# Gate and up products of the feed-forward stages: one 512-column matmul over the tokens' high and low parts instead of two of 256

## What is computed

```python
def rmsnorm_2(x, g):
    xf = x.astype(jnp.float32)
    y = xf * lax.rsqrt(jnp.mean(xf * xf, axis=-1, keepdims=True) + EPS)
    return (y * g.astype(jnp.float32)).astype(x.dtype)

def swiglu(h, wg, wu, wd):
    return (jax.nn.silu(h @ wg) * (h @ wu)) @ wd

        # first block, w_ff1 1024 x 4096, w_ff2 4096 x 1024
        h = rmsnorm(x, norm_pre_ffn[l])
        f = jnp.square(jax.nn.relu(h @ w_ff1[l])) @ w_ff2[l]
        x = x + rmsnorm(f, norm_post_ffn[l])

    # second block, two layers; wg and wu 1024 x 2816, wd 2816 x 1024
    for i in range(DEPTH_2):
        x = x + 0.5 * swiglu(rmsnorm_2(x, ffn_norm1[i]), ffn1_wg[i], ffn1_wu[i], ffn1_wd[i])
        ...
        x = x + 0.5 * swiglu(rmsnorm_2(x, ffn_norm2[i]), ffn2_wg[i], ffn2_wu[i], ffn2_wd[i])
```

## Time and profile before

| | |
|---|---|
| three runs | 1329.15, 1333.12, 1334.98 us, median 1333.12 |
| the profiled execution | 1334.74 us, of which the profile's span is 1333.0 |
| mean granted TensorE clock | 0.971 of full speed |
| instructions in the span | 21173 |
| DMA | 221.65 MB, 166 GB/s over the span |

### The profile page before, as it was taken

How to read it: one execution, slowest core, us unless ns; L and a number is a source line. 1 busy time by engine, 2 the same in 40 slices (tenths; PEclk the granted TensorE clock), 3 DMA queues, 4 the chain that set the end, 5 groups by cost and what they waited for, 6 DMA issues and landing times.

```text
span 1333.0 us, 21173 instructions
## 1 busy us (share of the span) xinstructions
PE 1254.7 (94%) x8758; PEld 1157.2 (87%) x8758; DVE 785.3 (59%) x1019; ACT 603.7 (45%) x786; POOL 135.2 (10%) x165
## 2 busy tenths in 40 slices
PE   6897899999899999978999999999999778999998
PEld 6895899999799999856999999999998667999997
DVE  4786465555565555664655555755555674655554
ACT  5456433333443444564433334534444683533442
POOL 4431100000400000340100000100001430100000
PEclk9897999999999999978999999999999898999999
DMA  9972255556375556440465555555553321455530
GB/s 310 331 198 96 64 191 187 187 186 202 132 232 187 188 189 190 158 151 19 144 205 182 183 188 189 166 188 189 189 177 113 125 64 66 159 189 187 189 126 32
DMA packets 167266, 221.65 MB, mean 166 GB/s; under 512 B 6056, under 2 KB 148460, under 8 KB 167068
## 3 DMA queue, kind: packets, MB, share of 16 engines
q1 hardware_dynamic: 164572, 212.28, 49.3%
q0 software_dynamic: 2624, 8.37, 1.9%
HBM read 213.26 MB, written 7.38 MB: 166 GB/s over the span
## 4 chain that ended last, share of the span: by engine, by line
PE 84%; DVE 7%; ACT 3%; issue 2%; SPq 1%; POOL 1%; DMA 1%; DVEq 0%; ACTq 0%
PE ps L244 26%; PE ps L245 26%; PE ps L246 26%; PE ps L527 2%; DMA raw<-in_w_in 1%; DVE w_lo L225 1%; PE ps L540 1%; PE ps L552 1%; POOL scratch L757 1%; DVE arena L617 1%; ACT w_hi L218 1%; PE ps L363 0%; DVE scratch L764 0%; DVE h_lo L416 0%; ACT h_hi L408 0%
## 5 line engine op out<-in xcount | busy, mean ns | idle before, releaser
L225 DVE TENSOR_TENSOR w_lo<-raw,w_hi 128x2048 fp32r<-128x2048 f32 x194 | 441.3, 2275 | 286.7 <-ACT w_hi L218 286.7
L218 ACT CAST w_hi<-raw 128x2048 fp32r<-128x2048 f32 x197 | 373.7, 1898 | 473.6 <-PE ps L246 459.5
L244 PE MATMUL ps<-h_hi,w_hi 128*128 128x256 f32 x1744 | 495.5, 284 | 8.3 <-DVE h_lo L416 8.3
L245 PE MATMUL ps<-h_lo,w_hi 128*128 128x256 f32 x1744 | 494.2, 283 | 0.0
L246 PE MATMUL ps<-h_hi,w_lo 128*128 128x256 f32 x1744 | 494.1, 283 | 0.0
L244 PEld LDWEIGHTS ps<-h_hi,w_hi 128*128 128x128 f32 x1744 | 335.1, 192 | 11.8 <-issue 7.0
L245 PEld LDWEIGHTS ps<-h_lo,w_hi 128*128 128x128 f32 x1744 | 335.2, 192 | 2.1
L246 PEld LDWEIGHTS ps<-h_hi,w_lo 128*128 128x128 f32 x1744 | 335.2, 192 | 0.0
L244 PE MATMUL ps<-w_hi,act_hi 128*128 128x512 f32 x480 | 187.5, 391 | 1.4 <-DVE act_lo L989 1.4
L245 PE MATMUL ps<-w_lo,act_hi 128*128 128x512 f32 x480 | 187.4, 390 | 0.0
L246 PE MATMUL ps<-w_hi,act_lo 128*128 128x512 f32 x480 | 186.7, 389 | 0.0
(11 more groups left out here) (230 smaller groups left out, 965.8 us busy)
## 6 DMA issues: line engine op xcount, KB each, us to landing
raw<-in_ffn_wg SPq DMA_DIRECT2D x44, 1024.0 KB, 5.3
raw<-in_ffn_wu SPq DMA_DIRECT2D x44, 1024.0 KB, 5.3
raw<-in_ffn_wd SPq DMA_DIRECT2D x44, 1024.0 KB, 4.9
raw<-in_w_ff SPq DMA_DIRECT2D x32, 1024.0 KB, 5.3
raw<-in_w_in SPq DMA_DIRECT2D x8, 1024.0 KB, 15.0
raw<-in_a_w_in SPq DMA_DIRECT2D x5, 1024.0 KB, 5.5
canvas<-act POOLq DMA_DIRECT2D x6, 688.0 KB, 12.1
raw<-in_w_out SPq DMA_DIRECT2D x4, 1024.0 KB, 6.5
```

The costliest lines, as they stand in the source:

```text
L218: nc.scalar.copy(w_hi[:, b % RING, 0:n], raw[:, b % RAW, 0:n]).then_inc(hi_ready, 1)
L225: nc.vector.tensor_tensor(w_lo[:, b % RING, 0:n], raw[:, b % RAW, 0:n], w_hi[:, b % RING, 0:n].bitcast(F32), ALU.subtract).then_inc(lo_rea ...
L244: nc.tensor.matmul(to, still[0], moving[0], start=start, stop=False, skip_group_check=True)
L245: nc.tensor.matmul(to, still[0], moving[1], start=False, stop=False, skip_group_check=True)
```

## The change

`h_hi` and `h_lo` become the two halves of one tile `h_both`, so that for each slice k of the width the high and low parts of the 256 tokens lie side by side, 512 columns. A new `wide_features_out` takes the place of `features_out` in F0 to F4: one matmul of 512 columns with the weights' high part, which writes high x high to the bank's first half and high x low to its second, and one of 256 columns with the weights' low part, added to the first half. A block's two feature halves now fill two whole banks: F0's products and all gates go to banks 0 and 1, all ups to banks 2 and 3, and neither has a second buffer. A new `sum_halves` on VectorE adds the two halves of both banks into SBUF. `times_row` multiplies in place in SBUF. The next product into a pair of banks waits for the sum (`relu_summed`, `gate_summed`, `upper_summed`). `row_tensor` writes to bank 4, and in SwiGLU stages stands behind the gate product of step 0.

```diff
-        h_hi = sb("h_hi", [P, KD, TOK], F32R)
-        h_lo = sb("h_lo", [P, KD, TOK], F32R)
+        h_both = sb("h_both", [P, KD, 2, TOK], F32R)
+        h_hi, h_lo = h_both[:, :, 0, :], h_both[:, :, 1, :]
...
+        def wide_features_out(b, bank, turn=0, wait_h=None):
+
+            nc.tensor.wait_ge(lo_ready, b + 1 + RAW * turn)
+            hi, lo = parts(b)
+            for f in range(2):
+                for k in range(KD):
+                    if wait_h is not None and f == 0 and k % 2 == 0:
+                        nc.tensor.wait_ge(h_lo_ready, wait_h + k // 2 + 1)
+                    nc.tensor.matmul(ps[:, bank + f, :], hi[:, k, f * P:(f + 1) * P], h_both[:, k, :, :].rearrange("p a b -> p (a b)"),
+                                     start=k == 0, stop=False, skip_group_check=True)
+                    last = nc.tensor.matmul(ps[:, bank + f, 0:TOK], lo[:, k, f * P:(f + 1) * P], h_both[:, k, 0, :],
+                                            start=False, stop=k == KD - 1, skip_group_check=True)
+            last.then_inc(block_used, 1)
+
+        def sum_halves(to, bank):
+            return nc.vector.tensor_reduce(to.rearrange("p (f t) -> p f t", f=2),
+                                           ps[:, bank:bank + 2, :].rearrange("p f (h t) -> p f t h", h=2), AX.X, ALU.add)
...
-        def times_row(to, bank):
-            return nc.vector.tensor_tensor(to.rearrange("p (f t) -> p f t", f=2), ps[:, bank, :].rearrange("p (f t) -> p f t", f=2),
-                                           row_of_both, ALU.mult)
+        def times_row(tile):
+            halves_of = tile.rearrange("p (f t) -> p f t", f=2)
+            return nc.vector.tensor_tensor(halves_of, halves_of, row_of_both, ALU.mult)
...
         def relu_tensor(s, turn=0):
-            if s >= 3:
-                nc.tensor.wait_ge(hidden_ready["F0"], s - 2 + 3 * turn)
-            features_out(b_up(s), hidden_bank(s % 3), turn=turn, wait_h=8 if s == 0 else None)
+            if s:
+                nc.tensor.wait_ge(relu_summed, s + 3 * turn)
+            wide_features_out(b_up(s), 0, turn=turn, wait_h=8 if s == 0 else None)
...
         def relu_vector(s, turn=0):
             nc.vector.wait_ge(block_used, b_up(s) + 1 + RAW * turn)
-            times_row(scaled[:, s % 3, :], s % 3).then_inc(relu_scaled, 1)
+            sum_halves(scaled[:, s % 3, :], 0).then_inc(relu_summed, 1)
+            nc.vector.wait_ge(relu_summed, s + 1 + 3 * turn)
+            times_row(scaled[:, s % 3, :]).then_inc(relu_scaled, 1)
...
         def swiglu_tensor(st, n, s, turn=0):
-            if s >= 2:
-                nc.tensor.wait_ge(hidden_ready[st], s - 1 + 2 * turn)
-            features_out(b_gate(st, s), hidden_bank(s % 2), turn=turn, wait_h=4 * n if s == 0 else None)
+            if s:
+                nc.tensor.wait_ge(gate_summed, steps_ahead[st] + s + 2 * turn)
+            wide_features_out(b_gate(st, s), 0, turn=turn, wait_h=4 * n if s == 0 else None)
+            if s == 0:
+                row_tensor(n)
+            if s:
+                nc.tensor.wait_ge(upper_summed, steps_ahead[st] + s + 2 * turn)
+            wide_features_out(b_upper(st, s), 2, turn=turn)
             if s == 1:
                 nc.tensor.wait_ge(row_ready, FEED[n] + 1)
-            features_out(b_upper(st, s), hidden_bank(2 + s % 2), turn=turn)
-            if s == 0:
-                row_tensor(n)
...
         def swiglu_vector(st, s, turn=0):
             nc.vector.wait_ge(block_used, b_gate(st, s) + 1 + RAW * turn)
-            times_row(gate[:, s % 2, :], s % 2).then_inc(gate_scaled[st], 1)
+            sum_halves(gate[:, s % 2, :], 0).then_inc(gate_summed, 1)
+            nc.vector.wait_ge(gate_summed, steps_ahead[st] + s + 1 + 2 * turn)
+            times_row(gate[:, s % 2, :]).then_inc(gate_scaled[st], 1)
             split_block(b_gate(st, s) + 3, turn)
...
             nc.vector.wait_ge(block_used, b_upper(st, s) + 1 + RAW * turn)
+            sum_halves(upper[:, s % 2, :], 2).then_inc(upper_summed, 1)
             nc.vector.wait_ge(half_ready[st], s + 1 + 2 * turn)
-            nc.vector.scalar_tensor_tensor(act[:, s % 2, :], half_g[:, s % 2, :], 0.5, ps[:, 2 + s % 2, :],
+            nc.vector.wait_ge(upper_summed, steps_ahead[st] + s + 1 + 2 * turn)
+            nc.vector.scalar_tensor_tensor(act[:, s % 2, :], half_g[:, s % 2, :], 0.5, upper[:, s % 2, :],
                                            ALU.mult, ALU.mult).then_inc(hidden_ready[st], 1)
```

More of the change, by code:

```diff
@@ L387, in row_tensor @@
             for t in range(TT):
-                last = nc.tensor.matmul(ps[:, 3, t * P:(t + 1) * P], tri[:, 2 * P:3 * P], diag[:, t, :], start=True, stop=True, skip_group_check=True)
+                last = nc.tensor.matmul(ps[:, 4, t * P:(t + 1) * P], tri[:, 2 * P:3 * P], diag[:, t, :], start=True, stop=True, skip_group_check=True)
             last.then_inc(row_psum, 1)
@@ L392, in row_vector_copy @@
             nc.vector.wait_ge(row_psum, FEED[n] + 1)
-            nc.vector.tensor_copy(row[:, :], ps[:, 3, 0:TOK]).then_inc(row_ready, 1)
+            nc.vector.tensor_copy(row[:, :], ps[:, 4, 0:TOK]).then_inc(row_ready, 1)
             nc.vector.wait_ge(row_ready, FEED[n] + 1)
-        def times_row(to, bank):
-            return nc.vector.tensor_tensor(to.rearrange("p (f t) -> p f t", f=2), ps[:, bank, :].rearrange("p (f t) -> p f t", f=2),
-                                           row_of_both, ALU.mult)
+        def times_row(tile):
+            halves_of = tile.rearrange("p (f t) -> p f t", f=2)
+            return nc.vector.tensor_tensor(halves_of, halves_of, row_of_both, ALU.mult)
         def norm_gain(n, k):
@@ L958, in build @@
         gate_scaled = {st: sem(f"gate_scaled_{st}") for st in swiglu}
-        def hidden_bank(bank):
-            return lambda f: ps[:, bank, f * TOK:(f + 1) * TOK]
+        upper = carve(3072, 2, 512)
+        gate_summed = sem("gate_summed")
+        upper_summed = sem("upper_summed")
+        steps_ahead = {st: I1 * n for n, st in enumerate(swiglu)}
         def second_product(st, b, s, buf, begin, end, turn=0, per=0):
@@ L999, in relu_tensor @@
         def relu_tensor(s, turn=0):
-            if s >= 3:
-                nc.tensor.wait_ge(hidden_ready["F0"], s - 2 + 3 * turn)
-            features_out(b_up(s), hidden_bank(s % 3), turn=turn, wait_h=8 if s == 0 else None)
+            if s:
+                nc.tensor.wait_ge(relu_summed, s + 3 * turn)
+            wide_features_out(b_up(s), 0, turn=turn, wait_h=8 if s == 0 else None)
             if s == 0:
                 row_tensor(2)
+            if s == 1:
+                nc.tensor.wait_ge(row_ready, FEED[2] + 1)
             if s:
                 second_product("F0", b_down(s - 1), s - 1, (s - 1) % 3, s == 1, False, turn, 3)
+        relu_summed = sem("relu_summed")
         relu_scaled = sem("relu_scaled")
```

## The result

| | before | after |
|---|---|---|
| median (runs) | 1331.16 us (8 runs, 1327.2 to 1334.98) | 1324.94 us (8 runs, 1322.26 to 1326.73) |
| ratio | 1 | **0.9948** [0.9933, 0.9962] |
| the profiled execution: time, span | 1334.7, 1333.0 | 1326.62, 1324.9 |

The change makes the kernel 0.5% faster, 6 to 7 us, where I had 17.5. The time lies above my range of 1310 to 1323. The border that I drew for "faster", 0.5%, lies inside the interval of the ratio.

What follows compares the result with a forecast made beforehand. TensorE, busy throughout the SwiGLU stages, was taken as the bound. Matmuls -20.8, the stop at F0's step 1 +2.0 and F0's end +1.3 made -17.5 us, so 1316 us forecast from a median of 1333.1, range 1310 to 1323.

Steps and rivals of the forecast that it cites:

- What bounds the kernel: SwiGLU stages: TensorE is busy all 178 us of F2, so each ns less for a matmul is a ns less time.
- What a matmul costs: TensorE, full clock: two matmuls of 256 take 240.0 ns, one of 512 takes 227.5, so a pair saves 12.5 ns.
- Term 1: Matmuls of F0 to F4: 1664 pairs at 12.5 ns each give 20.8 us less.
- Rival 2: TensorE's pairs: the fixed part doesn't go with the matmul, a pair saves 2.5 ns; 1332 us; chance 0.04.
- Term 2: VectorE: 104 more reductions of 1.22 us each, between 0.82 and 2.3, hidden behind TensorE.
- rival 1: VectorE in F0: the reduction is slow, up to 2.3 us, and bounds F0; 1327 us; chance 0.09.
- Does it stay hidden: VectorE's sums fit under TensorE's steps; in F0 with 0.55 us to spare, unless a sum takes over 1.8 us.
- Term 3: F0 between steps 0 and 1: step 1 waits for step 0's sum, 2.0 us more; a clock drop kept for the range.
- Term 4: End of F0: the sum joins the chain that the last down product waits for, 1.3 us more.
- Nothing from the moved row of factors, nothing from DMA: F1 to F4: the moved row costs nothing; queues keep their order, loads come 2% more often.
- Rival 3: VectorE becomes the bound through a slow reduction, at 3.3 us some +15 us, 1348; chance 0.03.
- rival 4: Where stages hand over, DMA or ScalarE end last and TensorE's gain is given back; 1327 with two thirds; chance 0.03.

Runs made afterwards that it cites:

- e1: The changed kernel with each block's 16 matmuls of 512 columns ahead of its 16 of 256; 1320.78 us, 0.9907 of before.
- e2: The changed kernel with two matmuls of 512 columns ahead of two of 256, in place of by turns; 1315.45 us, 0.9882 of before.
- e5: The changed kernel with the low weights' matmul made 512 columns wide too, a price list and not a version; 1491.65 us in one execution.
- e6: The changed kernel with each sum of halves made twice, the first into a spare tile; 1333.27 us in one execution.
- e4: The changed kernel with step 1 of F0 in banks 2 and 3, so it needn't wait for step 0's sum; 1321.27 us, 0.9912 of before.
- e7: e4's edit, plus F0's last step splitting its up block behind the hidden features, against the changed kernel; 1317.34 us, 0.9883 of before.

## Why the prediction was wrong, point by point

**What bounds the kernel: right.** In F2 TensorE is busy for 178 of 178 us at clock 1.00, in after as in before. Each ns of a matmul was a ns of the step.

**What a matmul costs: this step failed.** It is the sentence "two matmuls of 256 take 240.0 ns, and one of 512 columns 227.5: 12.5 ns less for each pair". Both prices were taken from runs of matmuls of one size, and the change never runs one size twice. A pair takes 352.4 to 354 ns for 347.5, and saves 5.9 ns by the step for 12.5. Term 1 is then 1664 x 5.9 ns = 9.9 us, not 20.8: **10.9 us too much**. e1 and e2 put the same matmuls in runs, and there the prediction's 16.58 us stands in the timeline.

**Rival 2 was right in kind**, at two thirds of its size (6.6 ns of the 12.5 lost, where it had 10): "a 512 followed by a 256 takes nearly what three of 256 took". I gave it 0.04 because the 512-column stretch pays the same fixed part as the 256-column one. That speaks of a stretch, not of a change of size, and the rival's own remark that no row alternates the sizes should have put the low end of the saving, 2.5 ns or so, into the range. The reason it gave, a change of weights that costs more behind a longer matmul, fell with e5 and e2: the weights change as often there, behind matmuls of 512 columns too, and the starts are 226.7 ns apart in the one, a pair 347.7 ns in the other. The Trainium skill's rule ("TensorE: Matmul & The Clock Gate", Back-to-back issue gap), 2.5 ns beside N / 2.4, would make a pair save 2.5 ns; the 5.9 measured lie between it and the 12.5 that I took from the trace. Neither speaks of a change of size. The same section gives this rule for an isolated matmul, which the prediction leaves out, and has about 131 ns for one of 512 columns in a stream with weight loads; no row here shows that, the nearest being 226.7 ns.

**Term 2, the reduction: right.** 1.225 us for 1.22, for pairs that lie 1 KB apart in PSUM. The Trainium skill's full rate for one stream that writes a word for two read ("Vector Engine (DVE) Microarchitecture Reference", Measured stream behaviour on trn2) is what the trace shows; its 1.73 ns an element for a hopping source isn't seen here, and rival 1 fell with it. "Does it stay hidden": right as well, in F0 with 0.76 us to spare, where I had 0.55. The limit of 1.8 us was too low. It took 9.23 us for the rest of the chain; e6 has 259.32 - 250.31 = 9.01 and the sums' own 2.39, so that a sum of up to 11.11 - 9.01 = 2.1 us fits.

**Term 3, step 1 of F0: right as idle time (2.0 us for 2.0), wrong in that the clock was left out of the sum.** I kept 1.5 us "for the range", and for one stop. In the profiled execution F0 has 6.8 us more at half clock than before's, and the way to F1 with F1 another 6.8. Half of F0's 6.8 is 3.4 us, and F0's account closes: 16 x 0.11 = -1.8 for the steps, +1.8 and +1.3 for the stops, +3.4 for the clock, +4.7 for +4.6 found. F1 gives 0.7 us for 2.4. So **about 5 us** were missing in the sum for that execution. F0's part, 3.4 us, goes with the stops, as e4 and e7 show; F1's 1.7 us may or may not, as the table under e7 tells. What the clock costs in the mean of many executions isn't shown either: e2 has both stops and yet a median of 1315.45 us (four runs, 1312.5 to 1322.8), which is my forecast.

**Term 4, the end of F0: right**, 2.70 us of wait where 1.44 stood. The last down product of F0 in after:

```profile
343.52 0.50 PE L244 MATMUL ps<-w_hi,act_hi 128*128 128x512 f32 x1 [2.70 <-DVE act_lo L1009]
```

**Nothing from the moved row of factors, nothing from DMA: right.** No wait for either stands among TensorE's in F2 to F4, which agree within 0.1 us. Rival 3 (VectorE the bound) and rival 4 (handovers) didn't come, though a part of the clock's share is of rival 4's kind: it is paid where F0 hands over to F1.

The sum made again: -9.9 + 2.0 + 1.3 + about 5 is -1.6 us; the stages F0 to F4 with the way to F1 give -3.2 (steps somewhat shorter at the ends of stages, and MA, M1 and MB apart). The medians have -6.2 and the ratio's interval -5.1 to -8.9. What lies between is in M1, MA and MB, -5.2 us in these two executions, where the stretches at half clock vary; that the change moves them in the mean is neither shown nor excluded. So in this execution the time came out as near to my range as it did partly by luck: without those 5.2 us it would have been some 3 us below before's.

## What to carry to other kernels

Read a matmul's price from a stretch that has the same sequence of sizes as the new code; a price from a run of one size is the low end, not the value. Where an operand allows wider matmuls for a part of the work only, put the wide and the narrow ones in twos, or in eights and more: here this was worth another 0.2 us in 16.8, while fours gave only half of it. Why is open, so try more than one group size. Count a stop of some 2 us in a dense stream of matmuls as about twice its length until a window behind it shows the clock at 1.00 (F0 in e4: 3.6 us for a stop of 1.8 to 2.0), and give the first tile of a stage a bank of its own before giving one to its steady steps.

## What was not expected of the hardware

- Matmuls of 512 and 256 columns by turns: 235.7 and 116.7 ns from start to start, where runs of one size have 226.7 and 120.0. In groups of 2, 4, 8 and 16 a pair takes 347.7, 350.8, 348.5 and 347.3 ns, by turns 354.1.
- Behind a change from 256 to 512 columns it takes some five matmuls until the starts are 227 ns apart (234, 236, 229, 232 and 231 ns in the down product of before).
- Stops of 1.8 and 2.7 us in an otherwise dense stream stand ahead of stretches at half clock (0.74 and 0.82 granted in the windows behind them). The one behind step 1 goes when the stop goes; the second window is at 1.00 in e2 with the stop, and in e7 without it.
- A tensor_reduce over two elements 1 KB apart in PSUM takes 1.225 us for 1024 elements; one of 1024 elements in SBUF takes 1.220.
